# Moving eight VectorE preparation steps of the second head pair: six into the softmax rounds of the first attention part, two onto GpSimd

## The chip, the cores and the metric

The kernel runs on one core of one Trainium2 chip. The metric is the device time of that core in microseconds; smaller is better. Before the change three runs gave 2102.01, 2103.89 and 2096.85 us, a median of 2102.01 us. The execution that the profiler recorded took 2102.01 us, and its trace spans 2100.2 us.

## The reference, cut to what matters

The program is one step of a two-layer backbone over 512 latent tokens and 128 context tokens (T = 640 columns in all), everything in fp32. In each layer one input projection feeds three groups of heads: windowed attention, an RWKV-7 scan in both directions, and a Fourier mix. Then come an output projection and a feed-forward part. The change touches how the operands of the RWKV scan are prepared:

```
kk = k * rwkv_k_k;  kk = kk * rsqrt(sum(kk*kk) + 1e-12)
for d in (forward, backward):
    k_d = k * (1 + (a_d - 1) * k_a)
    S   = S * w_t - (S kk_t)(kk_t * a_t) + v_t k_t          # one step of the scan
    y_t = S r_t
```

The scan is done in chunks of 64 tokens. For that, the running sum of the log decay is turned into exponentials, and these are multiplied into r, kk, k_d and kk*a for all 640 tokens and both directions before any chunk is treated.

## The kernel before, in words

**Queues.** Each engine has a stream of instructions written out by hand, one function per engine (`@block.tensor`, `@block.vector` and so on), run strictly in the order written. The streams meet only at semaphores: `ready`, `taken` and `wait_ge` in the text are waits. `own.after` makes an engine wait for its own instruction.

**The stage around the change.** In each layer, after the projections, the order is: the preparation of head pair 0 (`prep(0, ...)` on VectorE), attention part A (eight rounds, `attention(0, NATT_A, 1)`), `recurrence(0)`, attention part B (twelve rounds), `recurrence(1)`. Head pair 1's preparation `prep(1, 0..12)` is spread over this: steps 0 to 2 before attention A, steps 3 and 4 inside its rounds 1 and 2 (table `between`), and steps 5 to 12 inside `recurrence(0)`. Steps 7 to 12 are one instruction each over 128 x 1280 elements; step 6 is one over the same size with a scalar operand; step 5 is five tiny ones. The exponentials of head pair 1 that steps 5 onwards need are computed by ScalarE in rounds 3 to 5 of attention A (`prep_exp`).

**A round of attention.** TensorE computes the scores of round m, the transposes of round m-1 and the values of round m-2. VectorE does `softmax_in(m)` (a copy of two elements, L1747, then two reductions from PSUM, L1749), `normalise(m-3)` (L1769, L1770) and `inverse(m-1)` (L1756, L1759). ScalarE takes the exponential of round m, then copies the transposes of round m-1. VectorE's loop has three more turns than there are rounds (turns and rounds are counted from 0), and `normalise` of the last round stands in the last turn.

**The recurrence.** `recurrence(ht)` on TensorE starts with waits: for all `normalise` of the attention part before it (`o_sb`), for `scaled_ready` and `ar_done` of its head pair, and for the states loaded by DMA. It then goes through three groups of 4, 4 and 2 pairs of token tiles. Per group: transposes (L1048 to L1051), products (L1057 to L1063), masks on VectorE (L1799, L1801, L1806), five levels of matmul (L1085, L1092, L1097) with one VectorE mask per pair and level (L1814) and one ScalarE copy (L1480), then the final products, L1823 to L1827 on VectorE, and the chain of states.

**GpSimd.** `by_r_and_rate(t)` multiplies head pair t's rows by r and by kk (L684, L685) and signals `ar_done`. Before the change it was called for t = 0 alone; head pair 1's two products were VectorE's steps 11 and 12. `state_in(t)` starts the DMAs of the states.

Of the kernel before, what the change touches and what calls it, by code (L numbers as in the profile page):

```python
# [10 lines left out]
T = NL + NC_  # L11
# [231 lines left out]
def build(nc, I, O):  # L243
# [5 lines left out]
    MUL, ADD, SUB, MAX = ALU.mult, ALU.add, ALU.subtract, ALU.max  # L249
    ctx = ExitStack()  # L250
    with ctx:
# [86 lines left out]
        ush = rows(0, 9)  # L338
# [45 lines left out]
        rate = (KK, KK1)  # L384
# [49 lines left out]
        ar_done = sig("ar_done", 2)  # L434
# [181 lines left out]
        def _(e):  # L616
            own = Own(e, pool_own)
# [14 lines left out]
            for l in range(DEPTH):  # L632
# [44 lines left out]
                def by_r_and_rate(t):  # L677

                    e.wait_ge(exps_ready.sem, exps_ready.upto(l, t + 1))
                    taken(e, l, ("kinv", t))  # L680
                    rb = ush[:, t:t + 1, :].to_broadcast([128, 2, T])
                    kb = rate[t].unsqueeze(1).to_broadcast([128, 2, T])
                    H, A_, R_, K_, B_ = row_of[t]
                    nc.gpsimd.tensor_tensor(H[:, R_:R_ + 2, :], H[:, R_:R_ + 2, :], rb, MUL)  # L684
                    nc.gpsimd.tensor_tensor(H[:, A_:A_ + 2, :], H[:, A_:A_ + 2, :], kb, MUL).then_inc(ar_done(), 1)  # L685

                state_in(0)
                by_r_and_rate(0)
                state_in(1)

                for t in range(2):
# [857 lines left out]
        def _(e):  # L1549
            own = Own(e, dve_own)  # L1550
            V = nc.vector
# [48 lines left out]
            for l in range(DEPTH):  # L1600
# [49 lines left out]
                def prep(t, step):  # L1650

                    c0 = CC[:, 0, :].rearrange("p (c t) -> p c t", t=CH)
                    c1 = CC[:, 1, :].rearrange("p (c t) -> p c t", t=CH)
                    n = NCH
                    H, A_, R_, K_, B_ = row_of[t]
                    a_, k_ = (h[:, 6:8, :], CC) if t == 0 else (a1, h1[:, 6:8, :])
                    if step == 0:
                        taken(e, l, ("w", t, 0))
                        taken(e, l, ("w", t, 1))

                        V.tensor_tensor_scan(CC[:, 0, :], reset[:, :], S2[:, 0, :], 0.0, MUL, ADD)
                        own.after(V.tensor_tensor_scan(CC[:, 1, :], reset[:, :], S2[:, 1, :], 0.0, MUL, ADD))
                    elif step == 1:
                        V.tensor_copy(end[:, 0, :].unsqueeze(2), c0[:, :, 63:64])
                        V.tensor_copy(mid[:, 0, :].unsqueeze(2), c0[:, :, 31:32])
                        own.after(V.tensor_copy(end[:, 1, :].unsqueeze(2), c1[:, :, 63:64]))

                        own.after(V.tensor_tensor(CC[:, 1, :], S2[:, 1, :], CC[:, 1, :], SUB))
                    elif step == 2:
                        own.after(V.tensor_tensor(c1, c1, end[:, 1, :].unsqueeze(2).to_broadcast([128, NCH, CH]), ADD))  # L1670
                        own.after(V.tensor_copy(mid[:, 1, :].unsqueeze(2), c1[:, :, 32:33]))
                    elif step == 3:
                        own.after(V.tensor_tensor(chunks(CC), chunks(CC),
                                                  mid[:, :, :].rearrange("p a c -> p (a c)").unsqueeze(2).to_broadcast(
                                                      [128, 2 * NCH, CH]), SUB))
                    elif step == 4:
                        own.after(V.tensor_tensor(end[:, :, :], end[:, :, :], mid[:, :, :], SUB))
                        V.tensor_tensor(S2, CC, S2, SUB).then_inc(cum_ready(), 1)
                    elif step == 5:

                        e.wait_ge(exps_ready.sem, exps_ready.upto(l, t + 1))
                        V.tensor_tensor(dec[:, t, 0, 0:n - 1], eend[:, 0, 0:n - 1], emid[:, t, 0, 1:n], MUL)
                        V.tensor_copy(dec[:, t, 0, n - 1:n], eend[:, 0, n - 1:n])
                        V.tensor_copy(dec[:, t, 1, 0:1], eend[:, 1, 0:1])
                        own.after(V.tensor_tensor(dec[:, t, 1, 1:n], eend[:, 1, 1:n], emid[:, t, 1, 0:n - 1], MUL))
                        V.tensor_copy(dec[:, t, 1, LCH:LCH + 1], eend[:, 1, LCH:LCH + 1])
                    elif step == 6:

                        own.after(V.tensor_scalar(k_, a_, par[:, PR_KA + t:PR_KA + t + 1], omka[:, t:t + 1], MUL, ADD))
                    elif step == 7:  # L1690
                        own.after(V.tensor_tensor(k_, k_, ush[:, 2 + t:3 + t, :].to_broadcast([128, 2, T]), MUL))
                    elif step == 8:
                        own.after(V.tensor_tensor(a_, a_, H[:, 4:6, :], MUL))
                    elif step == 9:
                        own.after(V.tensor_tensor(H[:, K_:K_ + 2, :], H[:, 4:6, :], k_, MUL))
                    elif step == 10:
                        last = V.scalar_tensor_tensor(H[:, B_:B_ + 2, :], a_, -1.0,
                                                      rate[t].unsqueeze(1).to_broadcast([128, 2, T]), MUL, MUL)
                        last.then_inc(scaled_ready(), 1)
                        e.wait_ge(scaled_ready.sem, scaled_ready.upto(l, t + 1))  # L1700
                    elif step == 11:
                        own.after(V.tensor_tensor(H[:, R_:R_ + 2, :], H[:, R_:R_ + 2, :],
                                                  ush[:, t:t + 1, :].to_broadcast([128, 2, T]), MUL))
                    elif step == 12:
                        V.tensor_tensor(H[:, A_:A_ + 2, :], H[:, A_:A_ + 2, :],
                                        rate[t].unsqueeze(1).to_broadcast([128, 2, T]), MUL).then_inc(ar_done(), 1)

                def rate_inverse(t):
                    taken(e, l, ("kk", t))
# [28 lines left out]
                def attention(first, last_pair, t):  # L1738
# [30 lines left out]
                        own.after(V.tensor_copy(inv_row[:, m % 2, :], bank[:, 128:256]))  # L1769
                        V.tensor_tensor(qt[:, j, 128 * b:128 * b + 128], bank[:, 0:128], inv_row[:, m % 2, :], MUL).then_inc(o_sb(), 1)  # L1770

                    between = [(), (3,), (4,)]
                    for m in range(first, last_pair + 3):
                        if m < last_pair:
                            softmax_in(m)
# [14 lines left out]
                def recurrence(ht):  # L1790
                    for g, group in enumerate(GROUPS):
                        base = pair_index(ht, g, 0)
                        ng = len(group)
                        if ht == 0 and g == 0:
                            prep(1, 5)
                            prep(1, 6)
                        for n, (p, d, t) in enumerate(group):
                            e.wait_ge(prod_ps.sem, prod_ps.upto(l, base + n + 1))
                            V.tensor_tensor(P1[p], PS[:, 2 * p:2 * p + 2, 256:320],  # L1799
# [5 lines left out]
                            e.wait_ge(l0_sb.sem, l0_sb.upto(l, base + n + 1))  # L1805
                            V.tensor_tensor(T0[p], P1[p], eye64[:, :].unsqueeze(1).to_broadcast([128, 2, 64]),  # L1806
                                            ADD).then_inc(t0_sb(), 1)
                        if ht == 0:
                            prep(1, 7 + 2 * g)
                        for lv in range(1, 6):  # L1810
                            at = 5 * base + (lv - 1) * ng
                            for n, (p, d, t) in enumerate(group):
# [1 line left out]
                                V.tensor_tensor(P1[p], ps[2 * p][:, 0:128].rearrange("p (a t) -> p a t", a=2),  # L1814
                                                lvl[:, d, lv:lv + 1, :].to_broadcast([128, 2, 64]), MUL).then_inc(
                                                    p1_sb(), 1)
                        if ht == 0:
                            prep(1, 8 + 2 * g)
                        for n, (p, d, t) in enumerate(group):
                            e.wait_ge(qmn_ps.sem, qmn_ps.upto(l, base + n + 1))  # L1820
                            c = slice(128 * t, 128 * t + 128)
# [189 lines left out]
```

## Time and profile before

| | |
|---|---|
| median of 3 runs | 2102.01 us |
| the profiled execution, its span | 2102.01 us, 2100.2 us |
| TensorE matmul busy | 1967.7 us (94%) |
| VectorE, ScalarE, GpSimd busy | 792.9 (38%), 617.2 (29%), 480.6 us (23%) |
| layer 0: attention A, recurrence(0) | 247 to 277 us, 277 to 361 us |
| layer 0: attention B, recurrence(1) | 361 to 396 us, 396 to 482 us |
| layer 1 | the same stage some 1018 us later |

The busy shares are averages over stages with different limits. The feed-forward stages fill most of the span with TensorE alone; the stage around the change is a chain of short steps between TensorE, ScalarE and VectorE, and there the timeline must be read. In the timeline a row is: start, duration, engine, line, operation, output<-input, shape, count, and in brackets how long the engine was idle before it and which instruction released it. The printed duration of a VectorE instruction runs a little into the next one's start, so the sums below go from start to start.

### The profile page before, as it was taken

The numbers are of one execution on the slowest core, as the hardware profiler recorded it, in microseconds if no ns is written. First come the engines' busy times: TensorE is split into PE (matmuls) and PEld (weight loads), VectorE is DVE, ScalarE is ACT, GpSimd is POOL, SyncE is SP. The second block draws the span as 40 slices with busy tenths as digits, with TensorE's granted clock in tenths as the row PEclk, the third lists the DMA queues.
The fourth block names the chain that finished last, engine by engine and source line by source line (L and its number), as shares of the span: only waits on it lengthen the run. The fifth ranks groups of instructions, "written<-read, shape, count | busy, mean of one in ns | idle before, by whom it ended". The sixth has DMA issues, their size and how long they took to land.

```text
span 2100.2 us, 45861 instructions
## 1 busy us (share of the span) xinstructions
PE 1967.7 (94%) x20575; PEld 1761.8 (84%) x20575; DVE 792.9 (38%) x1707; ACT 617.2 (29%) x1226; POOL 480.6 (23%) x235
## 2 busy tenths in 40 slices
PE   6999898989989999999989998999898999999995
PEld 3998587885589999999989867869657999999995
DVE  1522865543153321333153256564414332133312
ACT  3423653631131111121133246354103211121112
POOL 1233300000033333333322440000002333333330
PEclk7999999999999999999999999999899999999998
DMA  9474100003152132222337513000022212222211
GB/s 321 156 208 141 62 4 5 2 4 102 62 141 77 46 90 81 81 68 70 95 101 199 155 48 63 4 4 4 3 61 61 81 52 80 82 79 75 66 32 51
DMA packets 238039, 163.45 MB, mean 78 GB/s; under 512 B 21634, under 2 KB 235380, under 8 KB 237332
## 3 DMA queue, kind: packets, MB, share of 16 engines
q1 hardware_dynamic: 236404, 158.55, 26.0%
q8 instruction: 163, 2.67, 0.5%
q0 software_dynamic: 1440, 1.97, 0.3%
q14 instruction: 32, 0.26, 0.0%
HBM read 157.35 MB, written 3.15 MB: 76 GB/s over the span
## 4 chain that ended last, share of the span: by engine, by line
PE 85%; DVE 7%; ACT 4%; issue 2%; DMA 1%; SPq 1%; POOL 0%; DVEq 0%; ACTq 0%; POOLq 0%
PE PS L816 28%; PE PS L817 28%; PE PS L754 6%; PE PS L1092 2%; PE PS L1085 2%; PE PS L778 2%; PE PS L1097 2%; PE PS L755 1%; DVE mix L1801 1%; PE PS L738 1%; ACT mix L1439 1%; PE PS L999 1%; PE PS L1107 1%; PE PS L971 1%; PE PS L984 1%
## 5 line engine op out<-in xcount | busy, mean ns | idle before, releaser
L642 POOL TENSOR_TENSOR wsplit<-ring,wsplit 128x1024 fp32r<-128x1024 f32 (+1 forms) x120 | 323.9, 2700 | 785.8 <-ACT wsplit L1310 785.8
L816 PE MATMUL PS<-h_hi,wsplit 128*128 128x320 f32 x1408 | 427.0, 311 | 11.5 <-POOL wsplit L642 6.2
L817 PE MATMUL PS<-h_hi,wsplit 128*128 128x320 f32 x1408 | 425.9, 311 | 0.0
L1310 ACT ACTIVATE wsplit<-ring 128x1024 fp32r<-128x1024 f32 (+1 forms) x120 | 137.5, 1148 | 730.5 <-PE PS L817 723.9
L816 PEld LDWEIGHTS PS<-h_hi,wsplit 128*128 128x128 f32 x1408 | 266.3, 189 | 12.8 <-issue 8.8
L817 PEld LDWEIGHTS PS<-h_hi,wsplit 128*128 128x128 f32 x1408 | 266.5, 189 | 0.0
L817 PE MATMUL PS<-h_lo,wsplit 128*128 128x320 f32 x704 | 217.1, 309 | 0.0
L816 PE MATMUL PS<-h_lo,wsplit 128*128 128x320 f32 x704 | 217.1, 309 | 0.0
L816 PE MATMUL PS<-hid_hi,wsplit 128*128 128x320 f32 x704 | 213.3, 311 | 0.0
L817 PE MATMUL PS<-hid_hi,wsplit 128*128 128x320 f32 x704 | 211.9, 309 | 0.0
L1896 DVE SCALAR_TENSOR_TENSOR x<-PS,mod,x 128x128 f32<-128x128 f32 (+2 forms) x128 | 52.5, 462 | 394.8 <-PE PS L817 263.6
L816 PE MATMUL PS<-in_hi,win 128*128 128x320 f32 x544 | 170.2, 321 | 6.9 <-ACT in_hi L1284 4.6
L817 PE MATMUL PS<-in_hi,win 128*128 128x320 f32 x544 | 166.5, 314 | 0.0
L816 PEld LDWEIGHTS PS<-hid_hi,wsplit 128*128 128x128 f32 x704 | 132.1, 188 | 3.0 <-issue 3.0
L754 PE MATMUL PS<-mix,ring 128*128 128x512 f32 x256 | 132.2, 598 | 0.9 <-DVE mix L1888 0.9
L817 PEld LDWEIGHTS PS<-hid_hi,wsplit 128*128 128x128 f32 x704 | 132.2, 188 | 0.0
L817 PEld LDWEIGHTS PS<-h_lo,wsplit 128*128 128x128 f32 x704 | 132.2, 188 | 0.0
L816 PEld LDWEIGHTS PS<-h_lo,wsplit 128*128 128x128 f32 x704 | 132.1, 188 | 0.0
L642 POOL TENSOR_TENSOR win<-ring,win 128x1024 fp32r<-128x1024 f32 x34 | 81.7, 2404 | 219.1 <-ACT win L1310 218.9
L1916 DVE TENSOR_TENSOR hid_lo<-tmp,hid_hi 128x640 fp32r<-128x640 f32 x44 | 127.8, 2905 | 1.5
L1480 ACT ACTIVATE mix<-PS 128x256 f32<-128x256 f32 x240 | 92.3, 384 | 121.1 <-PE PS L1097 53.7
L816 PEld LDWEIGHTS PS<-in_hi,win 128*128 128x128 f32 x544 | 104.6, 192 | 17.9 <-issue 11.6
(315 smaller groups left out, 3527.9 us busy)
## 6 DMA issues: line engine op xcount, KB each, us to landing
ring<-in_w_ada SPq DMA_DIRECT2D x48, 1024.0 KB, 7.5
ring<-in_ffn_w_in SPq DMA_DIRECT2D x88, 512.0 KB, 5.0
ring<-in_ffn_w_out SPq DMA_DIRECT2D x32, 704.0 KB, 4.5
ring<-in_w_in SPq DMA_DIRECT2D x8, 1024.0 KB, 5.9
ring<-in_w_in SPq DMA_DIRECT2D x10, 512.0 KB, 8.8
ring<-in_w_in SPq DMA_DIRECT2D x16, 256.0 KB, 6.5
ring<-in_w_out SPq DMA_DIRECT2D x16, 256.0 KB, 6.4
ring<-in_w_out SPq DMA_DIRECT2D x8, 512.0 KB, 7.8
```

The lines of the kernel that those rows point to most:

```text
L642: nc.gpsimd.tensor_tensor(lo, raw_w, hi, SUB).then_inc(wl_ready(), 1)
L754: mm(lat[:, :], w, v[:, 0:NL], start=(k == 0), stop=(k == n - 1))
L778: last = mm(bank[c:c + 32, at:at + 256], csil[:, k, :], w[:, k, :], start=(k < 4), stop=(k >= KT - 4))
L816: mm(lat[:, 0:TH], w, v[:, 0:TH], start=(n == 0), stop=(n == total - 1))
L817: last = mm(cx[:, 0:TH], w, v[:, TH:T], start=(n == 0), stop=(n == total - 1))
L1085: last = mm(ps[2 * p][cs, 64 * hd:64 * hd + 64], LP[p][cs, hd, BA, :], XY[p][cs, 2 + hd, :], start=True, stop=True)
L1092: mm(b1[cs, 64 * hd:64 * hd + 64], P1[p][cs, hd, :], XY[p][cs, hd, :], start=False, stop=(lv == 5), skip_group_check=True)
L1097: last = mm(b1[cs, at_x], XY[p][cs, hd, :], P1[p][cs, hd, :], start=False, stop=(lv == 4), skip_group_check=True)
L1310: act(hi, raw_w, ACT.Copy).then_inc(wh_ready(), 1)
L1480: act(XY[p].rearrange("p a t -> p (a t)"), ps[2 * p + 1][:, 0:256], ACT.Copy).then_inc(xy_sb(), 1)
L1896: last = V.scalar_tensor_tensor(x[:, m, a:b], bank[:, at:at + b - a], mod[:, gate_at + m, s:s + 1], x[:, m, a:b], MUL, ADD)
L1916: V.tensor_tensor(hid_lo[:, i % FH, :], tmp[:, :], hid_hi[:, i % FH, :], SUB).then_inc(hid_split(), 1)
```

## The change

Four edits. The two calls that head pair 1's steps 11 and 12 made on VectorE are gone, and `by_r_and_rate(1)` on GpSimd does those products, right behind `by_r_and_rate(0)` and ahead of `state_in(1)`. Steps 5 to 10 leave `recurrence(0)` and go into attention A: steps 5 and 6 in turn 6 of the loop, 7 in turn 7, 8 in turn 8, and 9 and 10 in turn 9. In a turn they stand last, behind `softmax_in`, `normalise` and `inverse`. The change holds for both layers.

```
                 state_in(0)
                 by_r_and_rate(0)
+                by_r_and_rate(1)
                 state_in(1)
...
-                    elif step == 11:
-                        own.after(V.tensor_tensor(H[:, R_:R_ + 2, :], H[:, R_:R_ + 2, :],
-                                                  ush[:, t:t + 1, :].to_broadcast([128, 2, T]), MUL))
-                    elif step == 12:
-                        V.tensor_tensor(H[:, A_:A_ + 2, :], H[:, A_:A_ + 2, :],
-                                        rate[t].unsqueeze(1).to_broadcast([128, 2, T]), MUL).then_inc(ar_done(), 1)
...
-                    between = [(), (3,), (4,)]
+                    between = [(), (3,), (4,), (), (), (), (5, 6), (7,), (8,), (9, 10)]
...
-                        if ht == 0 and g == 0:
-                            prep(1, 5)
-                            prep(1, 6)
...
-                        if ht == 0:
-                            prep(1, 7 + 2 * g)
...
-                        if ht == 0:
-                            prep(1, 8 + 2 * g)
```

Where the instructions stand now is shown at three places. The first is VectorE at the end of attention A, before the change; L1769 and L1770 are `normalise`, L1756 and L1759 `inverse`, L1682 to L1689 steps 5 and 6, L1799 the first instruction of the recurrence.

```order
L1759 TENSOR_TENSOR mix<-mats,den 128x256
L1769 COPY mix<-PS 128x128
L1770 TENSOR_TENSOR mix<-PS,mix 128x128
L1769 COPY mix<-PS 128x128
L1770 TENSOR_TENSOR mix<-PS,mix 128x128
L1682 TENSOR_TENSOR dec<-eend,emid 128x9
L1683 COPY dec<-eend 128x1
L1684 COPY dec<-eend 128x1
L1685 TENSOR_TENSOR dec<-eend,emid 128x9
L1686 COPY dec<-eend 128x1
L1689 TENSOR_SCALAR mix<-mix,par,omka 128x1280
L1799 TENSOR_TENSOR mix<-PS,lvl 128x128
```

The same place after the change, from the `inverse` of turn 7 on; lines are those of the new file, where L1764 and L1765 are `normalise`, L1751 and L1754 `inverse`, and L1692, L1694, L1696, L1698 steps 7 to 10.

```order
L1692 TENSOR_TENSOR mix<-mix 128x1280
L1764 COPY mix<-PS 128x128
L1765 TENSOR_TENSOR mix<-PS,mix 128x128
L1751 RECIPROCAL den<-den 128x2
L1754 TENSOR_TENSOR mix<-mats,den 128x256
L1694 TENSOR_TENSOR mix<-mix 128x1280
L1764 COPY mix<-PS 128x128
L1765 TENSOR_TENSOR mix<-PS,mix 128x128
L1696 TENSOR_TENSOR mix<-mix 128x1280
L1698 SCALAR_TENSOR_TENSOR mix<-mix 128x1280
L1764 COPY mix<-PS 128x128
L1765 TENSOR_TENSOR mix<-PS,mix 128x128
```

So steps 7 to 10 now stand ahead of the last three `normalise`, and two of them directly ahead of the last one, on which TensorE's start of the recurrence waits.

The second place is VectorE inside group 0 of `recurrence(0)`, before and with its change.

```order
L1806 TENSOR_TENSOR mix<-mix,eye 128x128
L1691 TENSOR_TENSOR mix<-mix 128x1280
L1814 TENSOR_TENSOR mix<-PS,lvl 128x128 x20
L1693 TENSOR_TENSOR mix<-mix 128x1280
L1823 TENSOR_TENSOR MN<-PS,eye 128x128
```

```order
L1798 TENSOR_TENSOR mix<-mix,eye 128x128
L1804 TENSOR_TENSOR mix<-PS,lvl 128x128 x20
L1811 TENSOR_TENSOR MN<-PS,eye 128x128
L1813 TENSOR_TENSOR mix<-PS,h 128x128
L1815 TENSOR_TENSOR MN<-PS,dec 128x128
```

The large products ahead of and behind the 20 level masks are gone; the same holds in groups 1 and 2. The third place is GpSimd, from the states of head pair 0 on, before the change and after it (L674 loads a state, L695 and L696 store one).

```order
L674 DMA s0in<-in_state_rwkv 64x64 x4
L684 TENSOR_TENSOR h<-h,mix 128x1280
L685 TENSOR_TENSOR h<-h,mix 128x1280
L674 DMA s0in<-in_state_rwkv 64x64 x4
L695 DMA out_new_s<-mix 64x64 x8
```

```order
L674 DMA s0in<-in_state_rwkv 64x64 x4
L684 TENSOR_TENSOR h<-h,mix 128x1280
L685 TENSOR_TENSOR h<-h,mix 128x1280
L684 TENSOR_TENSOR mix<-mix 128x1280
L685 TENSOR_TENSOR mix<-mix 128x1280
L674 DMA s0in<-in_state_rwkv 64x64 x4
L696 DMA out_new_s<-mix 64x64 x8
```

The two rows whose operands are both in `mix` are new: the products of head pair 1. They wait for head pair 1's exponentials, and nothing else on GpSimd moved.

## Rows read from the trace of the kernel before

**Rows 1.** Timeline of TensorE, end of attention A, start of recurrence(0).
```profile
276.10 0.39 PE L1003 MATMUL PS<-mix,ones 128*64 128x128 f32 x4
277.36 0.31 PE L1034 MATMUL PS<-mats,s0in 64*128 64x64 f32 x2 [0.87 <-issue]
277.59 0.33 PE L1048 MATMUL PS<-mats,h 128*128 128x128 f32 x1
```
**Rows 2.** Timeline of VectorE, turns 5 to 10 of attention A.
```profile
264.97 0.42 DVE L1759 TENSOR_TENSOR mix<-mats,den 128x256 f32<-128x256 f32 x1
...
270.01 0.17 DVE L1747 COPY mix<-nsink 128x2 f32<-128x2 f32 x1 [1.12 <-PE PS L971]
...
271.44 0.29 DVE L1769 COPY mix<-PS 128x128 f32<-128x128 f32 x1
...
272.50 0.28 DVE L1769 COPY mix<-PS 128x128 f32<-128x128 f32 x1
...
275.44 0.29 DVE L1769 COPY mix<-PS 128x128 f32<-128x128 f32 x1 [1.80 <-PE PS L1003]
...
277.06 0.16 DVE L1682 TENSOR_TENSOR dec<-eend,emid 128x9 f32<-128x9 f32 x1
...
277.53 0.94 DVE L1689 TENSOR_SCALAR mix<-mix,par,omka 128x1280 f32<-128x1280 f32 x1
```
**Rows 3.** Timeline of VectorE, recurrence(0), group 0.
```profile
280.41 0.29 DVE L1799 TENSOR_TENSOR mix<-PS,lvl 128x128 f32<-128x128 f32 x1 [1.95 <-PE PS L1063]
...
284.41 1.48 DVE L1691 TENSOR_TENSOR mix<-mix 128x1280 f32<-128x1280 f32 x1
285.93 0.88 DVE L1814 TENSOR_TENSOR mix<-PS,lvl 128x128 f32<-128x128 f32 x4
...
302.14 0.29 DVE L1823 TENSOR_TENSOR MN<-PS,eye 128x128 f32<-128x128 f32 x1 [2.71 <-PE PS L1124]
```
**Rows 4.** Timeline of VectorE, recurrence(1), group 0, which has no such steps.
```profile
399.12 0.29 DVE L1799 TENSOR_TENSOR mix<-PS,lvl 128x128 f32<-128x128 f32 x1 [3.19 <-PE PS L1063]
...
404.29 0.99 DVE L1814 TENSOR_TENSOR mix<-PS,lvl 128x128 f32<-128x128 f32 x4 [1.10 <-PE PS L1085]
...
420.53 0.29 DVE L1823 TENSOR_TENSOR MN<-PS,eye 128x128 f32<-128x128 f32 x1 [4.04 <-PE PS L1124]
```
**Rows 5.** Timeline of GpSimd, the products of head pair 0.
```profile
227.56 2.88 POOL L684 TENSOR_TENSOR h<-h,mix 128x1280 f32<-128x1280 f32 x1 [5.39 <-ACT h L1405]
230.40 2.45 POOL L685 TENSOR_TENSOR h<-h,mix 128x1280 f32<-128x1280 f32 x1
```
**Rows 6.** Timeline of VectorE beside them.
```profile
227.61 2.86 DVE L1682 TENSOR_TENSOR dec<-eend,emid 128x9 f32<-128x9 f32 x1 [2.16 <-ACT h L1405]
230.39 0.14 DVE L1683 COPY dec<-eend 128x1 f32<-128x1 f32 x1
```
**Rows 7.** Timeline of ScalarE, the last exponential of head pair 1.
```profile
263.17 1.27 ACT L1405 ACTIVATE mix<-mix 128x1280 f32<-128x1280 f32 x1
```
**Rows 8.** Timeline of GpSimd at 211 us.
```profile
211.34 1.61 POOL L665 TENSOR_TENSOR mix<-mix 128x640 f32<-128x640 f32 x1
```
**Rows 9.** Timeline of VectorE at 211 us, two copies of ten elements.
```profile
211.66 1.33 DVE L1664 COPY end<-mix 128x10 f32<-128x10 f32 x1
212.90 0.16 DVE L1665 COPY mid<-mix 128x10 f32<-128x10 f32 x1
```
**Rows 10.** Timeline of TensorE, start of attention A.
```profile
247.50 0.70 PE L971 MATMUL PS<-mix 64*128 64x256 f32 x4 [2.13 <-ACT mix L1384]
```
**Rows 11.** Stretches: length, busy PE, PEld, DVE, ACT, POOL, granted clock, DMA.
```profile
248.00:252.00 4.00, 3.67 (x24) 2.91 (x23) 3.28 (x13) 3.12 (x10) 0.00 (x0) 0.57 1.10 350
424.70:431.50 6.80, 6.21 (x68) 5.56 (x67) 2.37 (x10) 1.83 (x4) 0.00 (x0) 0.57 0.01 2
```
**Rows 12.** Timeline of TensorE, recurrence(1), start of group 1.
```profile
427.78 0.45 PE L1048 MATMUL PS<-mats,mix 128*128 128x128 f32 x1 [0.47 <-DVE mix L1851]
```
**Rows 13.** Timeline of VectorE, the same place.
```profile
432.72 0.29 DVE L1799 TENSOR_TENSOR mix<-PS,lvl 128x128 f32<-128x128 f32 x1 [5.09 <-PE PS L1063]
```

## The prediction, made before the changed kernel had run

> **What bounds the kernel now.** I read the busy times of the page first, which stand in the table above: TensorE 94% of the span, VectorE 38%. That average comes from the projection and feed-forward stages and says little on this stage, which is a chain over three engines, so I went to the timelines of TensorE and VectorE between attention A and the end of recurrence(1), layer 0. Layer 1 repeats it, so all sums below are per layer and then doubled.
>
> Three things are to be seen. First, TensorE's last matmul of attention A starts at 276.10 and the first of the recurrence at 277.36, after an idle 0.87 us that is called issue [rows 1]. In the code that first matmul waits for the last `normalise`, and VectorE's timeline bears that out: the two last `normalise` end at 277.06, right where L1682, step 5, begins [rows 2]. So VectorE's last turn of attention A releases recurrence(0); whatever stands ahead of it in VectorE's queue delays the recurrence by its full length once VectorE's idle time there is used up. Second, that idle time is small: 1.12 us before turn 7, and 1.80 us before turn 9 [rows 2]. Third, in the recurrence VectorE has room: it sat idle 1.95 us behind steps 5 and 6, and 2.71 us behind step 8 [rows 2, 3].
>
> **What the removal gives back.** Steps 5 and 6 took 277.06 to 278.47 [rows 2] and the next instruction waited for TensorE until 280.41 [rows 3]: nothing. Step 8 hides behind the last products of the group, and so do 10 and 12, which stand in the same place of groups 1 and 2: nothing. Steps 7, 9 and 11 stand between the first masks and the level masks. What they cost can be read off, since recurrence(1) is the same work without them. From L1799 to the first L1814 it is 5.52 us with step 7 (280.41 to 285.93) and 5.17 us without (399.12 to 404.29); over the group, L1799 to L1823, 21.73 and 21.41 us [rows 3, 4]. So a step of 1.52 us costs 0.32 us there, since TensorE and ScalarE are not yet ready for the level masks. Three such steps give 3 x 0.32 = 0.96 us. Bounds: nothing below, 3 x 1.52 = 4.6 us above if all of each were on the path; the row pair says 0.32 and I take that.
>
> **What the additions cost.** I write VectorE's queue out from its free moment behind the `inverse` of turn 6, 270.01 - 1.12 = 268.9. Durations, start to start: steps 5 and 6 together 1.41; a `softmax_in` 1.43 (270.01 to 271.44); a `normalise` with an `inverse` 1.06 (271.44 to 272.50), each half of it; a large step 1.52 (284.41 to 285.93) [rows 2, 3]. Then: steps 5 and 6 to 270.3; turn 7's softmax, normalise, inverse to 272.8; step 7 to 274.3; turn 8's normalise and inverse to 275.4; step 8 to 276.9; turn 9's normalise to 277.4; steps 9 and 10 to 280.5; the last normalise to 281.0. Before it was 277.06. The tail costs 3.9 us, although 7.5 us of work was put in, as the 1.80 us gap and smaller ones take up the rest. TensorE is not late in this: values(7) started its last part at 276.10 and needs the `inverse` that now ends at 275.4.
>
> **What GpSimd's two new products do.** They wait for the last exponential, which ends at 263.17 + 1.27 = 264.44 [rows 7], start then at about 264.5, and take 2.84 and 2.45 us, like those of head pair 0 [rows 5]: 264.5 to 267.4 and 267.4 to 269.8. Their own end is not urgent, since recurrence(1) needs them at 396 us. But they run beside attention A. Where head pair 0's products ran, a VectorE product of nine elements, 0.16 us long when alone [rows 2], took 2.86 us and ended with GpSimd's instruction, and the one-element copy behind it ran in 0.14 us [rows 6]. At 211 us a copy of ten elements took 1.33 us and ended with GpSimd's product, 212.99 and 212.95 [rows 8, 9]. So while GpSimd reads two operands, VectorE instructions with two operands in SBUF are held to its end, and some small copies too. In turn 5 `inverse` (L1759, two SBUF operands) starts at 264.97 [rows 2], 0.4 us behind GpSimd's start, and is held to about 267.7. Next is turn 6's copy of two elements (L1747), by then behind the second product. No row shows a two-element copy beside GpSimd; the nearest rows are the ten-element copy (held) and the one-element copy (free). Free, it goes on at 267.7, and only that turn's `inverse` is held, to 270.1 instead of 268.9: 1.2 us more. Held, turn 6 starts at 269.8: 1.43 + 1.06 to 272.3, steps 5 and 6 to 273.8 instead of 270.3: 3.5 us more. I take held, since L1747 takes 0.17 us, closer to the 0.16 us of a ten-element copy alone [rows 9] than to the 0.14 us of the one-element one. The start of recurrence(0) is then late by 3.9 + 3.5 = 7.4 us, with bounds of 3.9 (GpSimd disturbs nothing) and 8.5 (it is also slowed by VectorE and holds a third instruction, one more 1.1 us).
>
> The Trainium skill (SBUF — State Buffer, section "Who interferes with whom") has the pair of ports that VectorE and GpSimd share as an exclusive lock: whoever starts first holds it for its whole instruction, against VectorE instructions with two SBUF inputs and against copies in a two-port mode. The nine-element row agrees. By VectorE: DVE Perf Modes, section "Mode 2×_2P", a copy within SBUF gets into that mode if its outermost dimension is even: two elements do, one does not. By this rule the stall is the 3.5 us; were the rule wrong for so small a copy, it would be 1.2 us. It speaks against moving work to GpSimd beside attention.
>
> **What the clock adds.** After 2.13 us of idle before 247.50 TensorE's granted clock was 0.57 in 248 to 252 us [rows 10, 11], that is mostly 1.2 instead of 2.4 GHz. Now TensorE idles from about 281 (its last values, some 4 us later than before) to 284.7, right ahead of sixteen transposes. The start of a group took 2.82 us from the first transpose to L1799 at the full level (277.59 to 280.41) [rows 1, 3] and 4.94 us (427.78 to 432.72) where the clock was 0.57 [rows 11 to 13]: 2.1 us more. Whether the low stretch lies just there I can't read; between 0 and 2.1 I take 1.3, nearer the upper end, as the idle is longer than the 2.13 us that sufficed.
>
> **Sum.** 7.4 - 0.96 + 1.3 = 7.7 us per layer, 15.5 us for two. The profiled execution's own time is 2102.01 us, which is also the median of the runs: 2117.5 us.
>
> **The rivals.**
> - *The two-element copy is free.* 3.9 + 1.2 - 0.96 + 1.3 = 5.4 per layer: 2112.9 us. For it: the one-element copy ran free. Against: the ten-element one didn't.
> - *GpSimd disturbs nothing here*, since its products come late or start just behind VectorE's. 3.9 - 0.96 + 1.3 = 4.2 per layer, 2110.5 us, and 2107.9 us if the clock holds too. For it: the order of start decides, and 0.4 us of shift would change it. Against: VectorE comes back with a product each turn, and GpSimd's two last 5.3 us.
> - *The large steps stood on the path of the recurrence* (faster). If VectorE's order there, not TensorE, set the pace, all six large steps would give back 6 x 1.52 = 9.1 us per layer against 3.9 of the tail: 5.2 x 2 = 10.4 us, 2091.6 us. It decides from the point where the six give back more than the tail costs, 3.9 us, or 0.65 us each. Against it: each of the three visible ones gives 0.32 us, and 2.71 us of idle follow the step behind the levels.
> - *The moved steps hide entirely* because TensorE waits for something later than the last `normalise`. Then only -0.96 x 2: 2100.1 us. Against it: L1034 starts 0.3 us behind that `normalise`, which is as short as such a wait gets here.
>
> **How the numbers follow.** Chances: copy held 0.57, copy free 0.18, GpSimd harmless 0.15, hidden entirely 0.07, faster by the recurrence 0.03. The lower end is 2108 (GpSimd harmless, clock full); the upper one is 8.5 + 2.1 - 0.96 = 9.6 per layer plus 1 us each for a low stretch within attention A where TensorE now idles too, 2102 + 21 = 2123. A change under 0.3% (6.3 us) can't be told from none. The first three cases all lie above 2108.3 but for the third's lower half: slower 0.57 + 0.18 + 0.11 = 0.86. No change: hidden entirely and the rest of the third, 0.07 + 0.04 = 0.11. Faster: 0.03.
>
> **What would show it.** Right: GpSimd L684 in attention A starts some 0.1 us behind the last exponential; L1754 (the new number of L1759) of turn 5 lasts over 2 us and the L1742 copy of turn 6 about 2 us; TensorE's L1034 of layer 0 starts near 284.7, with some 3 to 4 us idle ahead of it; L1799 to L1814 takes 5.2 us in recurrence(0) as in recurrence(1). Wrong: L1742 at 0.17 us throughout (second case), L1034 near 281 (third), or at 277 (fourth), or the levels of recurrence(0) faster than those of recurrence(1) ever were.

## The result and the profile after

The changed kernel took 2117.80 us (median of four runs, 2113.60 to 2119.42) against 2102.03 us of the kernel before (2096.85 to 2103.89) on the same chip: a ratio of 1.0076, 95% interval 1.0052 to 1.0099. It is slower, by 15.8 us. The forecast was 2117.5 us. Its profiled execution took 2116.57 us with a span of 2114.7 us, 14.6 us over that of before.

The page says little on this, as before. These are its busy times, with shares and instructions:

```profile
PE 1968.4 (93%) x20575; PEld 1763.4 (83%) x20575; DVE 797.8 (38%) x1703; ACT 617.5 (29%) x1226; POOL 492.1 (23%) x239
```

VectorE lost four large products and is still busy 5 us longer, since time in which an instruction is held counts as busy; GpSimd gained four and is busy 11.5 us longer. TensorE's work is the same. So the time went into waits, and I read the stage for them. GpSimd's timeline in attention A of layer 0 has the two new products:

```profile
264.33 2.91 POOL L684 TENSOR_TENSOR mix<-mix 128x1280 f32<-128x1280 f32 x1 [31.74 <-ACT mix L1406]
267.20 3.08 POOL L685 TENSOR_TENSOR mix<-mix 128x1280 f32<-128x1280 f32 x1
```

They start when the last exponential (L1406) ends. VectorE's timeline from there to the recurrence:

```profile
264.78 2.73 DVE L1754 TENSOR_TENSOR mix<-mats,den 128x256 f32<-128x256 f32 x1
267.44 2.86 DVE L1742 COPY mix<-nsink 128x2 f32<-128x2 f32 x1
270.22 0.74 DVE L1744 CUSTOM_DVE_ANT_0 mix<-PS,attmask,nsink 128x512 f32<-128x512 f32 x1
...
274.05 0.17 DVE L1742 COPY mix<-nsink 128x2 f32<-128x2 f32 x1
...
276.53 1.48 DVE L1692 TENSOR_TENSOR mix<-mix 128x1280 f32<-128x1280 f32 x1
...
279.11 1.48 DVE L1694 TENSOR_TENSOR mix<-mix 128x1280 f32<-128x1280 f32 x1
...
281.16 1.48 DVE L1696 TENSOR_TENSOR mix<-mix 128x1280 f32<-128x1280 f32 x1
282.68 1.49 DVE L1698 SCALAR_TENSOR_TENSOR mix<-mix 128x1280 f32<-128x1280 f32 x1
284.20 0.29 DVE L1764 COPY mix<-PS 128x128 f32<-128x128 f32 x1
284.52 0.29 DVE L1765 TENSOR_TENSOR mix<-PS,mix 128x128 f32<-128x128 f32 x1
289.62 0.29 DVE L1791 TENSOR_TENSOR mix<-PS,lvl 128x128 f32<-128x128 f32 x1 [4.81 <-PE PS L1064]
```

Two instructions that took 0.42 and 0.17 us before [rows 2] take 2.73 and 2.86: each ends within 0.3 us of the GpSimd product beside it (267.51 against 267.24, 270.30 against 270.28). Behind them not one gap is left: the idle 1.12 and 1.80 us of [rows 2] are used up, and each large step pushes the last `normalise` (L1764, L1765) back. TensorE's timeline shows who waits for it:

```profile
273.15 1.94 PE L985 MATMUL PS<-mats,mix 128*128 128x128 f32 x8 [3.43 <-ACT mix L1451]
...
280.97 0.39 PE L1004 MATMUL PS<-mix,ones 128*64 128x128 f32 x4
285.02 0.30 PE L1035 MATMUL PS<-mats,s0in 64*128 64x64 f32 x2 [3.67 <-issue]
```

Its values are done at 281.4 and the recurrence begins at 285.02; in [rows 1] the gap was 0.87 us. The profile calls the wait "issue" in both, so only the code (the wait for the last `normalise`) and VectorE's row, ending 0.2 us ahead, tell whose it is.

TensorE also waited 3.43 us inside the rounds, for the transposes behind the held softmax, and from 273.1 to 279.0 its granted clock was 0.54. That delays nothing here: from 264.4 to 284.8 VectorE has no idle time at all, so VectorE's queue, and not TensorE, sets when the last `normalise` runs. (In [rows 2] it was TensorE that VectorE waited for, 1.80 us.)

The stretches of TensorE, first of the kernel before and then of the one after, give busy times and the granted clock (the last number but two): attention A, then from the recurrence's first matmul to VectorE's first mask, then the rest of recurrence(0).

```profile
247.50:277.40 29.90, 25.73 (x265) 20.25 (x266) 22.20 (x79) 22.73 (x54) 0.00 (x0) 0.94 0.23 73
277.40:280.40 3.00, 3.00 (x58) 2.77 (x62) 1.03 (x3) 2.58 (x6) 2.16 (x4) 1.00 0.07 20
280.40:360.10 79.70, 72.01 (x2224) 66.53 (x2216) 44.67 (x145) 30.05 (x76) 0.00 (x0) 1.00 0.02 4
```

```profile
247.30:285.00 37.70, 28.18 (x264) 22.43 (x265) 33.92 (x85) 22.68 (x54) 5.95 (x2) 0.86 0.18 57
285.00:289.60 4.60, 4.58 (x54) 4.20 (x58) 0.00 (x0) 2.92 (x6) 2.10 (x4) 0.63 0.06 20
289.60:368.60 79.00, 70.94 (x2230) 66.48 (x2221) 36.66 (x139) 30.13 (x76) 0.00 (x0) 1.00 0.01 4
```

Attention A is 7.9 us longer. The transposes and products that open the recurrence ran at the full 2.4 GHz before and now mostly at 1.2 GHz (granted 0.63), and take 4.6 us instead of 3.0. From the first mask on the recurrence is a little shorter.

Stage by stage, layer 0 / layer 1, in us. Attention A and the two recurrences are counted from their first matmul; a recurrence ends, and attention B begins, at the transposes of the recurrence's final states, some 0.85 us before the next stage's first matmul:

| kernel | attention A | recurrence(0) | attention B | recurrence(1) |
|---|---|---|---|---|
| before | 29.9 / 30.4 | 82.8 / 83.0 | 36.0 / 34.7 | 85.6 / 83.5 |
| after | 37.8 / 38.3 | 83.6 / 84.0 | 35.0 / 35.7 | 82.0 / 82.0 |
| after, a second profile | 37.7 / 37.9 | 83.9 / 83.0 | 35.1 / 34.7 | 82.1 / 82.1 |
| steps only (experiment 1) | 33.9 / 34.3 | 85.2 / 86.3 | 35.8 / 34.7 | 83.4 / 81.9 |
| GpSimd only (2) | 32.8 / 34.5 | 84.2 / 82.9 | 35.0 / 35.1 | 82.1 / 82.3 |
| single copies (3) | 36.3 / 36.4 | 83.1 / 85.0 | 36.2 / 35.0 | 83.3 / 82.8 |
| single copies, again | 36.3 / 36.2 | 84.7 / 85.3 | 35.3 / 35.0 | 81.7 / 82.4 |
| last two behind (4) | 34.9 / 35.2 | 82.9 / 82.5 | 35.0 / 34.8 | 84.0 / 83.7 |
| GpSimd in the levels (5) | 34.3 / 34.0 | 84.1 / 84.2 | 36.0 / 34.7 | 82.8 / 81.9 |
| all hidden (6) | 30.3 / 30.3 | 83.3 / 81.5 | 35.0 / 35.7 | 82.0 / 82.9 |

Attention A and recurrence(0) together are 8.7 and 8.8 us longer, 17.5 us for both layers. The rest of the program gives back some 3 us in balance: recurrence(1) is 3.6 and 1.5 us shorter, and in layer 0 the stretch at 0.57 of [rows 11, 12] is gone; on the other side the stretch between the two layers' stages, which the change doesn't touch, is 2.7 us longer than before (1.2 us in the second profile). The table also shows the noise: stages that two kernels have in common differ by 1 to 3 us from profile to profile. Attention A is the steady column, within 0.4 us between the two profiles of the changed kernel. The stage doesn't begin at the same time either: attention A of layer 0 starts between 247.3 and 250.1 us over the ten profiles, so rows of two kernels are to be compared from that start on.

### The profile page after: what moved, and what is told of

Read it like the earlier page. It is cut to its first block, busy times and chain, and to the rows that moved or that the text cites. A ratio compares the mean times of both kernels' runs of the same rounds, so it can differ in the third digit from the quotient of the medians.

```text
span 2114.7 us, 45851 instructions
## 1 busy us (share of the span) xinstructions
PE 1968.4 (93%) x20575; PEld 1763.4 (83%) x20575; DVE 797.8 (38%) x1703; ACT 617.5 (29%) x1226; POOL 492.1 (23%) x239
## 4 chain that ended last, share of the span: by engine, by line
PE 84%; DVE 8%; ACT 4%; issue 2%; DMA 1%; SPq 1%; POOL 0%; DVEq 0%; ACTq 0%; POOLq 0%
PE PS L817 28%; PE PS L818 28%; PE PS L755 6%; PE PS L1093 2%; PE PS L1086 2%; PE PS L779 2%; PE PS L1098 2%; PE PS L756 1%; DVE mix L1793 1%; ACT mix L1440 1%; PE PS L739 1%; PE PS L985 1%; PE PS L1108 1%; PE PS L1000 1%; PE PS L793 1%
## 5 line engine op out<-in xcount | busy, mean ns | idle before, releaser
L642 POOL TENSOR_TENSOR win<-ring,win 128x1024 fp32r<-128x1024 f32 x34 | 81.7, 2406 | 220.5 <-ACT win L1311 220.4
```

The source lines that it names most:

```text
L642: nc.gpsimd.tensor_tensor(lo, raw_w, hi, SUB).then_inc(wl_ready(), 1)
```

## The experiments

Experiments 1 to 4 ran together in three rounds, beside a before of 2101.70 us; the others together in five rounds, beside a before of 2099.26 us. In that second set the changed kernel itself took 2117.36 us (2113.15 to 2117.83), ratio 1.0080 [1.0063, 1.0096], for which this had been written:

> The changed kernel once more, beside the others of this group, so that the variant with one-element copies can be set against it on one chip: 2116 to 2119 us. In the first attention part, from its first matmul to the first of recurrence(0), 37.7 and 38.3 us as in its first profile, against 29.9 and 30.4 before.

It repeated the result, and its profile the stages of the first.

### 1. Steps 5 to 10 moved alone

The kernel before with the new table and its steps 11 and 12 kept on VectorE in group 2; GpSimd as before.

```
-                    between = [(), (3,), (4,)]
+                    between = [(), (3,), (4,), (), (), (), (5, 6), (7,), (8,), (9, 10)]
...
-                        if ht == 0:
-                            prep(1, 7 + 2 * g)
+                        if ht == 0 and g == 2:
+                            prep(1, 11)
```

> The kernel before with steps 5 to 10 moved into attention A as in the change, while steps 11 and 12 stay on VectorE in group 2 of recurrence(0). Theory (GpSimd's lock and the tail both count): turn 6 starts on time, the two-element copies take 0.17 us throughout, and only the tail is left: the first matmul of recurrence(0) is 3.9 us later than before, at about 281.3 in layer 0; 3.9 - 0.64 (two of the three hidden steps) + up to 2.1 for the clock, twice: 2109 to 2113 us, 2111 as value. Rival 1 (the whole rise is the tail, GpSimd plays no part): 2117 to 2118 us, recurrence(0) starting near 285. Rival 2 (the whole rise is GpSimd's): 2101 us.

Measured: 2110.87 us (2109.28 to 2114.40), ratio 1.0051 [1.0031, 1.0071], as expected. Attention A is 4.1 and 3.9 us longer, against 3.9 forecast for the tail. VectorE and TensorE of that run, in time:

```profile
266.93 0.17 DVE L1747 COPY mix<-nsink 128x2 f32<-128x2 f32 x1 [0.93 <-PE PS L971]
...
281.34 0.29 DVE L1770 TENSOR_TENSOR mix<-PS,mix 128x128 f32<-128x128 f32 x1
286.98 0.29 DVE L1796 TENSOR_TENSOR mix<-PS,lvl 128x128 f32<-128x128 f32 x1 [5.35 <-PE PS L1063]
```

```profile
281.84 0.45 PE L1034 MATMUL PS<-mats,s0in 64*128 64x64 f32 x2 [4.51 <-issue]
```

Nothing is held, the copy takes 0.17 us, and yet TensorE idles 4.51 us. From its first matmul to the first mask it is then 5.14 us, where it was 3.05 [rows 1, 3], and recurrence(0) as a whole is 2.4 and 3.3 us longer although steps 5 to 10 have left it. The tail so costs more here than its length: the opening that follows TensorE's wait runs mostly at the low clock, which is 2.1 and 1.5 us of those 2.4 and 3.3. Of these 13.7 us the rest of the program gave back some 5.

### 2. GpSimd's products alone

The kernel before with `by_r_and_rate(1)` behind `by_r_and_rate(0)`, and no steps 11 and 12 on VectorE (`if ht == 0 and g < 2`).

> The kernel before with steps 11 and 12 alone moved to GpSimd, ahead of the states of head pair 1, as in the change; steps 5 to 10 stay in recurrence(0). Theory: turn 6's two-element copy is held to about 270.2 and TensorE's transposes of round 6 start near 273.1 instead of 269.8; what follows is then set by TensorE's own last rounds, which ended at 281.3 in the changed kernel, so recurrence(0) starts near 281.5 to 282, some 4.4 us late; minus 0.24 for group 2, plus up to 1 us of clock, twice: 2109 to 2113 us. Rival 1 (GpSimd plays no part): 2101.5 us, start at 277.4. Rival 2 (the start is held only by what VectorE has queued, and its gaps take the 3.5 us up): 2103 to 2105 us.

Measured: 2109.28 us (2106.29 to 2112.84), ratio 1.0036 [1.0018, 1.0054]. VectorE is held as in the changed kernel:

```profile
267.76 2.74 DVE L1760 TENSOR_TENSOR mix<-mats,den 128x256 f32<-128x256 f32 x1
270.42 2.86 DVE L1748 COPY mix<-nsink 128x2 f32<-128x2 f32 x1
```

Taking away 3 us of VectorE's work per layer and giving it to an idle engine made the kernel slower. Attention A is 3.0 and 4.1 us longer, where 4.4 had been expected. TensorE's timeline shows that it pays elsewhere:

```profile
276.12 1.11 PE L985 MATMUL PS<-mats,mix 128*128 128x128 f32 x8 [3.44 <-ACT mix L1451]
...
282.92 0.30 PE L1035 MATMUL PS<-mats,s0in 64*128 64x64 f32 x2 [0.87 <-issue]
```

It waits 3.44 us inside the rounds, for the copy of the transposes that belong to the held softmax, and only 0.87 us ahead of the recurrence, as in [rows 1]. Behind that wait of 3.44 us its granted clock was 1.00 (276.1 to 282.1), where behind the 3.43 us of the changed kernel it was 0.54: the length of the wait doesn't tell which of the two follows.

### 3. One-element copies

The changed kernel, with the copy of two elements written as two copies of one.

```
-                        V.tensor_copy(Pm[:, m % 3, :, 0:1], nsink[:, j:8:4].unsqueeze(2))
+                        for g in range(2):
+                            V.tensor_copy(Pm[:, m % 3, g, 0:1], nsink[:, 4 * g + j:4 * g + j + 1])
```

> The changed kernel with the two-element copy of each softmax round written as two copies of one element. Theory (a copy of two elements is held by GpSimd's product, one of one element is not): turn 6 starts at about 267.6, its reductions run beside GpSimd's second product, only the product with two SBUF operands in that turn's inverse is held; recurrence(0) starts 2.3 us earlier than in the changed kernel, near 282.7, and twice 2.3 is 4.6 us: 2112 to 2114 us. Rival 1 (any copy within SBUF is held): 2118 us, the first of the two copies 2.9 us long. Rival 2 (the reductions are held too, as they read one SBUF operand): 2118 us, with a reduction of over 2 us.

Measured: 2118.53 us (2115.22 to 2118.82), ratio 1.0080 [1.0065, 1.0096]: no gain, against 2112 to 2114 us expected. But in VectorE's timeline the mechanism is as claimed:

```profile
267.73 2.70 DVE L1755 TENSOR_TENSOR mix<-mats,den 128x256 f32<-128x256 f32 x1
270.35 0.20 DVE L1743 COPY mix<-nsink 128x1 f32<-128x1 f32 x2
270.47 0.74 DVE L1745 CUSTOM_DVE_ANT_0 mix<-PS,attmask,nsink 128x512 f32<-128x512 f32 x1
...
272.52 0.96 DVE L1755 TENSOR_TENSOR mix<-mats,den 128x256 f32<-128x256 f32 x1
```

Beside it GpSimd's second product:

```profile
270.09 3.11 POOL L685 TENSOR_TENSOR mix<-mix 128x1280 f32<-128x1280 f32 x1
```

It runs to 273.2. Both copies take 0.20 us in its first part, and the reductions from PSUM keep their 0.74 us. Only the next product with two operands in SBUF is held, to 273.5, so part of the stall comes back in it. Attention A is 1.4 and 1.9 us shorter than in the changed kernel, and the time is not. The start of the recurrence in layer 0, TensorE and then VectorE:

```profile
286.33 0.30 PE L1035 MATMUL PS<-mats,s0in 64*128 64x64 f32 x2 [3.42 <-issue]
```

```profile
289.32 0.29 DVE L1792 TENSOR_TENSOR mix<-PS,lvl 128x128 f32<-128x128 f32 x1 [3.19 <-PE PS L1064]
```

After 3.42 us of idle this opening took 2.99 us at a granted clock of 1.00; the one of layer 1, after the same 3.42 us, took 5.39 at 0.50. In layer 0 the low stretch lay ahead of the wait, in TensorE's last values (0.59 from 279.7 to 281.7), where it cost VectorE 0.49 us. Since this left open whether the gain was lost or never there, the kernel ran again, side by side with the changed one:

> The changed kernel with one-element copies, again, with the changed kernel beside it. The first profile showed the attention part 1.5 and 1.9 us shorter than in the changed kernel, yet the time was no lower. Theory (the gain is real and was hidden by the scatter of the start and of the clock's low stretches): 2 to 4 us below the changed kernel here. Rival (the gain is given back later, since the recurrence that follows runs slower): within 1 us of the changed kernel, with the recurrence parts longer by what the attention part is shorter, in both profiles.

Measured: 2117.32 us (2116.54 to 2118.09), ratio 1.0082 [1.0067, 1.0098], the same as the 2117.36 us of the changed kernel. Attention A is 36.3 and 36.2 us (1.4 and 2.1 less than in the first profile of the changed kernel, 1.3 and 1.7 less than in the second), recurrence(0) 84.7 and 85.3 us (1.1 and 1.3 more, 0.8 and 2.3 more). TensorE's timeline in layer 0, VectorE's first mask and the stretch between them show where part of that is:

```profile
280.13 0.39 PE L1004 MATMUL PS<-mix,ones 128*64 128x128 f32 x4
285.03 0.44 PE L1035 MATMUL PS<-mats,s0in 64*128 64x64 f32 x2 [4.52 <-issue]
```

```profile
290.19 0.29 DVE L1792 TENSOR_TENSOR mix<-PS,lvl 128x128 f32<-128x128 f32 x1 [5.37 <-PE PS L1064]
```

```profile
285.00:290.00 5.00, 4.97 (x46) 4.55 (x50) 0.00 (x0) 2.91 (x6) 2.10 (x4) 0.53 0.08 18
```

Counted from the start of attention A (248.72 here, 247.27 in the changed kernel), TensorE's values are done 2.3 us earlier and the recurrence begins 1.4 us earlier, so the idle time is 0.85 us longer. The granted clock of the opening is 0.53 instead of 0.63: it takes 5.16 us, 0.56 more than in the changed kernel. That is about half of what recurrence(0) of layer 0 took longer. In layer 1 the opening (5.38 us) is as long as in the first profile of the changed kernel (5.39), and all of the 1.3 us lies behind it: in group 1, 22.10 us from the first mask to the last products against 21.72, and between the groups, 6.60 and 6.65 against 6.27 and 6.07, all at a granted clock of 1.00. No row says why. So the mechanism, the held copy, is shown, and the time says that the gain is lost; that recurrence(0) regularly gives it back is not shown, since in the first profile recurrence(0) of layer 0 was 0.5 us shorter, not longer. Its cause stays open.

### 4. Steps 9 and 10 behind the last normalise

The changed kernel, with an empty turn 9 and its two steps in a turn 10, behind the last `normalise`.

```
-                    between = [(), (3,), (4,), (), (), (), (5, 6), (7,), (8,), (9, 10)]
+                    between = [(), (3,), (4,), (), (), (), (5, 6), (7,), (8,), (), (9, 10)]
```

> The changed kernel with steps 9 and 10 one turn later, so that they stand behind the last normalise instead of ahead of it. Theory (the last normalise releases recurrence(0)): it ends 3.04 us earlier, the first matmul of recurrence(0) is at about 282.0, and the two steps end at 284.9, where the first masks of the recurrence are not due before 285; twice 3.04 us off 2117.8 is 2111.7 us, 2110 to 2113 with the clock. Rival (TensorE's start is set by something else, and VectorE's steps are hidden ahead of it): 2118 us.

Measured: 2111.59 us (2109.77 to 2113.07), ratio 1.0051 [1.0035, 1.0066], some 6 us below the changed kernel. VectorE's timeline at the end of attention A:

```profile
284.39 0.29 DVE L1765 TENSOR_TENSOR mix<-PS,mix 128x128 f32<-128x128 f32 x1
284.60 1.48 DVE L1696 TENSOR_TENSOR mix<-mix 128x1280 f32<-128x1280 f32 x1
286.12 1.49 DVE L1698 SCALAR_TENSOR_TENSOR mix<-mix 128x1280 f32<-128x1280 f32 x1
287.94 0.29 DVE L1791 TENSOR_TENSOR mix<-PS,lvl 128x128 f32<-128x128 f32 x1 [0.34 <-PE PS L1064]
```

The two steps now run while TensorE opens the recurrence, and end 0.34 us before the first mask could start. (Attention A begins at 250.02 here, 2.8 us later than in the changed kernel.) Attention A is 2.9 and 3.1 us shorter than in the changed kernel, which is the full length of both steps: those two alone were some 40% of the loss. TensorE waits only 1.47 and 0.88 us, and both openings run at the full clock, 3.05 us. That the total came out at the 2111.7 us expected from the two steps alone is in part scatter: recurrence(0) is 0.7 and 1.5 us shorter as well, and recurrence(1), whose work is the same, 2.1 and 1.6 us longer.

### 5. GpSimd's products beside the levels

The changed kernel, with `by_r_and_rate(1)` held back until the masks of group 0 are under way. The new wait makes it do so.

```
                 by_r_and_rate(0)
-                by_r_and_rate(1)
                 state_in(1)
+                e.wait_ge(p1_sb.sem, p1_sb.upto(l, 4))
+                by_r_and_rate(1)
```

> The changed kernel with GpSimd's two products of head pair 1 held back until the first level masks of group 0 of recurrence(0) are done, where VectorE runs only instructions with one operand in SBUF. Theory: attention A takes 4.0 us more than before, as with the steps alone, not 7.9; the products run beside the levels and hold nothing; 3.9 - 0.96 + 1 to 2 us of clock, twice: 2108 to 2112 us, 2110 as value. Rival (GpSimd's products hold any VectorE instruction that reads SBUF): level masks of over 2 us in group 0 of recurrence(0), 2113 to 2118 us.

Measured: 2111.80 us (2108.23 to 2112.29), ratio 1.0053 [1.0036, 1.0071], within the 2108 to 2112 expected. Attention A is 34.3 and 34.0 us, that of experiment 1. GpSimd, then VectorE in the same stretch:

```profile
293.95 2.89 POOL L684 TENSOR_TENSOR mix<-mix 128x1280 f32<-128x1280 f32 x1 [7.97 <-DVE mix L1805]
296.81 2.90 POOL L685 TENSOR_TENSOR mix<-mix 128x1280 f32<-128x1280 f32 x1
```

```profile
295.68 0.99 DVE L1805 TENSOR_TENSOR mix<-PS,lvl 128x128 f32<-128x128 f32 x4 [1.81 <-PE PS L1087]
298.48 0.99 DVE L1805 TENSOR_TENSOR mix<-PS,lvl 128x128 f32<-128x128 f32 x4 [1.81 <-PE PS L1087]
```

Four masks in 0.99 us, as in [rows 4]: instructions that read one operand from PSUM aren't held at all. The same GpSimd work, 30 us later, costs nothing that can be seen.

### 6. Everything in idle places

The kernel before with experiment 5's place for GpSimd, step 7 behind 5 and 6 ahead of the first masks, steps 8 and 9 behind the levels of group 0, and 10 behind those of group 1. This is the version to which the others point: it should keep the 0.32 us per step and pay for nothing.

```
                             prep(1, 6)
+                            prep(1, 7)
...
-                        if ht == 0:
-                            prep(1, 8 + 2 * g)
+                        for step in ((8, 9), (10,), ())[g] if ht == 0 else ():
+                            prep(1, step)
```

> A version meant to beat both: steps 5, 6 and 7 of head pair 1 right behind attention A where VectorE waits 1.95 us for the first products (7 needs 1.52), 8 and 9 behind the levels of group 0 where it waits 2.71 us more behind step 8, 10 behind those of group 1, and the last two products on GpSimd beside the levels of group 0. Theory: attention A as before (29.9 and 30.4 us), no large step between the masks and the levels, 0.96 us less per layer: 2099 to 2101 us, ratio 0.999. Rival 1 (the cost of those steps there was nothing, and 0.32 us was the clock): 2102 us. Rival 2 (the step behind the levels delays the last products of the group): 2103 to 2105 us.

Measured: 2101.47 us (2095.62 to 2104.70, 12 runs), ratio 1.0003 [0.9990, 1.0016]. VectorE, recurrence(0), group 0:

```profile
282.13 0.29 DVE L1802 TENSOR_TENSOR mix<-PS,lvl 128x128 f32<-128x128 f32 x1 [0.42 <-PE PS L1065]
...
287.31 0.99 DVE L1815 TENSOR_TENSOR mix<-PS,lvl 128x128 f32<-128x128 f32 x4 [1.10 <-PE PS L1087]
...
303.61 0.29 DVE L1824 TENSOR_TENSOR MN<-PS,eye 128x128 f32<-128x128 f32 x1 [1.18 <-PE PS L1126]
```

From the first mask to the levels it is 5.18 us and to the last products 21.48, nearly as in recurrence(1) in [rows 4]. The 0.34 us per step are there up to the levels; the 2 us that they add up to are not seen in the total, whose median is above the 2099 to 2101 expected and 2.2 above its own before (2099.26). The interval reaches from 2 us faster to 3 us slower, so this settles neither the theory nor its first rival. So no version here beats the kernel before by a measurable amount.

## Why the prediction was right, point by point

**What bounds the stage.** The last `normalise` releases recurrence(0): confirmed by the changed kernel (284.81 to 285.02) and by experiment 4, where only what stands ahead of it was changed and the start, counted from that of attention A, moved by that amount (34.9 and 35.2 us against 37.8 and 38.3).

**The removal.** Forecast were 0.32 us for each of three steps and 5.2 us from the first mask to the levels. In the changed kernel group 0 of layer 1, with the first row of the levels and the first of the last products, reads

```profile
1315.67 0.29 DVE L1791 TENSOR_TENSOR mix<-PS,lvl 128x128 f32<-128x128 f32 x1 [5.60 <-PE PS L1064]
...
1320.85 0.99 DVE L1804 TENSOR_TENSOR mix<-PS,lvl 128x128 f32<-128x128 f32 x4 [1.10 <-PE PS L1086]
...
1337.08 0.29 DVE L1811 TENSOR_TENSOR MN<-PS,eye 128x128 f32<-128x128 f32 x1 [4.04 <-PE PS L1125]
```

that is 5.18 and 21.41 us, the numbers of recurrence(1) before. Up to the levels the same holds for every group of both layers: 5.52 us became 5.18 in groups 0 and 1, and 3.52 became 3.18 in group 2, so three times 0.34. To the last products it is 0.3 us in group 0 and 0.24 in group 2; group 1 of recurrence(0) takes 21.5 to 23.0 us over the eight profiles without step 9 ahead of its levels, all at a granted clock of 1.00, and 21.7 to 22.7 us in the two with it, so what is left of the 0.34 us there can't be read. The rival in which large steps had stood on the recurrence's path falls with this.

**The tail, 3.9 us.** Experiment 1, alone: 4.1 and 3.9 us.

**GpSimd's hold, 3.5 us.** With it attention A is 7.9 and 7.9 us longer (forecast 7.4), and 3.8 and 4.0 us longer than in experiment 1. The 0.4 to 0.5 us above the forecast are covered by the second product, which took 3.08 us and not the 2.45 us of [rows 5]. The row I had read was that of head pair 0, with another tile as operand; experiment 5 has the same product as here with nothing held beside it, and it takes 2.90 us. The choice on which the term rested, that the two-element copy is held, is shown by both sides of it: 2.86 us in the changed kernel, 0.20 us for two one-element copies in experiment 3. The rival "copy free" had the right mechanism for another instruction and the wrong one for this. "GpSimd harmless" falls with experiment 2, as does "hidden entirely" with experiments 1 and 4. The Trainium skill (SBUF — State Buffer, section "Who interferes with whom") names the pair of ports that the two engines share, and by its VectorE: DVE Perf Modes, section "Mode 2×_2P", a copy within SBUF whose outermost dimension is even uses both of them. The trace agrees in all three kinds of instruction: two operands in SBUF held (2.73 us), one operand in PSUM not (0.99 us for four in experiment 5), a copy of two elements held and copies of one not.

**The clock, 1.3 us.** From the first matmul of the recurrence to the first mask: 4.60 us against 3.05 in layer 0 (285.02 to 289.62; [rows 1, 3]), so 1.55 us; in layer 1, where the start was at 1310.28, 5.39 us, after this idle time of TensorE:

```profile
1310.28 0.44 PE L1035 MATMUL PS<-mats,s0in 64*128 64x64 f32 x2 [4.45 <-issue]
```

That is 2.3 us more than the 3.06 of layer 1 before. The first is within the bounds of 0 to 2.1, the second just over them; in the second profile of the changed kernel both are 4.60 us. What I had not seen is that the tail alone brings it in full (experiment 1: 5.14 us). My reason for taking 1.3, that the idle would be longer than 2.13 us, is only half borne out. Over the twenty openings of recurrence(0) in the ten profiles, the eight behind an idle of 0.87 to 1.47 us ran at 1.00 and took 3.05 or 3.06 us; of the twelve behind 3.41 to 4.52 us eleven ran at 0.50 to 0.64 and took 4.52 to 5.39 us, and one, in experiment 3, ran at 1.00 and took 2.99. Among the twelve a longer idle is not a slower opening: 2.99 and 5.39 us both stand behind 3.42 us, 4.52 us behind 4.52. So that a low stretch follows such a wait was foreseen; its size, between 0 and 2.3 us, is chance as far as these runs show.

**The sum.** Forecast 7.7 us per layer; measured over the two stages 8.7 and 8.8. Of the 1 us more, 0.5 is attention A and 0.5 to 0.6 recurrence(0), which the clock's 1.55 and 2.3 us instead of 1.3 cover; in layer 1 they more than cover it, but there the opening of group 2, 3.10 us at 0.54 before, ran at the full clock in 2.17. That the total came out within 0.3 us of the forecast owes something to chance: the rest of the program gave back 3 us, mainly in recurrence(1) of layer 0, where the kernel before had a low stretch of the clock and the changed one has none. Whether the change caused that or such stretches fall by themselves, the runs don't settle; recurrence(1) of layer 0 is between 81.7 and 85.6 us over ten profiles, with identical work in it.

**Do the parts add up?** Experiments 1 and 2 lost 9.2 and 7.6 us against the before of their own set, 16.8 together, and the whole change 15.8. In attention A their 4.1 + 3.0 and 3.9 + 4.1 us make 7.1 and 8.0, against 7.9 and 7.9. Within the intervals of about 4 us either way this is additive, but in experiment 2 the hold was paid by TensorE's later rounds, with VectorE waiting for them, and in the changed kernel by VectorE's unbroken queue, so the agreement is no proof of it.

## What to carry to other kernels

Find the one instruction that releases the next stage and look at what stands ahead of it in its queue: work put there costs its full length once the gaps ahead are used up, and the same work directly behind it was free, as far as it fitted into the wait there (experiment 4). That GpSimd is idle doesn't make work given to it free; place it where VectorE reads from PSUM. And a gain of 1 to 2 us in one stage need not reach the total: in experiment 3 attention A was shorter in every profile and the time was the same, in part because openings ran at the low clock, in part for reasons that no row gives. Read the stages behind and the total, not only the one that was improved.

## What the runs showed of the hardware that was not expected

- Between two GpSimd products that follow each other, exactly one held VectorE instruction got through: L1754 ended at 267.51, the next (L1742) was held again for 2.86 us. So two products held two instructions, of 0.42 and 0.17 us alone.
- The second GpSimd product took 2.90 us with nothing held beside it (experiment 5), and 3.08 and 3.11 us where a VectorE product had been let through ahead of it. That the hold goes a little both ways would explain it, but isn't shown; head pair 0's second product, in the same position, took only 2.45 us [rows 5].
- The shape of a small copy decides: one of two elements was held for 2.86 us, two of one element each passed in 0.20 us together. A copy of three elements, which would part the number from its being even, was not run.
- TensorE idle for 0.87 us was followed by an opening of recurrence(0) at a granted clock of 1.00 each time; idle for 3.42 us, once by one at 1.00 and once by one at 0.50; idle for 4.52 us, by ones at 0.53 to 0.64. And once, in experiment 1, recurrence(1) of layer 0 opened at 0.65 after only 0.95 us of idle. In these runs the length of the idle before it doesn't by itself tell at which clock a stage opens.
